# Norms between the stages of a diffusion backbone: VectorE squares the last two tiles, the root's table and the second block's split go early, the spread uses two banks, and an FFN's first two blocks are taken tile by tile

## The chip, the cores and the metric

The kernel runs on one core of a Trainium2 chip. The metric is the device time of one execution in microseconds (us); the time of a kernel is the median of several executions.

## The reference

A backbone of two layers works on 256 context tokens and 256 latent tokens of width 1024. Each layer is: half-step SwiGLU FFN, token mixer, half-step SwiGLU FFN. The mixer is an S5 state-space layer in layer 0 and a gated DeltaNet (GDN) in layer 1. Before each sub-layer stands an RMSNorm with a modulation that depends on the condition, and the output is normed once more:

```python
def rms_norm(x, g):
    xf = x.astype(jnp.float32)
    return xf * lax.rsqrt(jnp.mean(xf * xf, axis=-1, keepdims=True) + EPS) * g.astype(jnp.float32)

def ada_norm(x, g, shift, scale):
    return rms_norm(x, g) * (1.0 + scale) + shift

def swiglu(h, w13, w2):
    a, b = jnp.split(h @ w13, 2, axis=-1)
    return (jax.nn.silu(a) * b) @ w2
...
        x = x + 0.5 * mx[:, 2] * swiglu(ada_norm(x, norm_g[i, 0], mx[:, 0], mx[:, 1]), ffn_w13[i, 0], ffn_w2[i, 0])
```

In the last layer the context tokens stop after the mixer's input, so norms 5 and 6 and the last FFN work on the 256 latent tokens alone. Everything is float32.

## The kernel before

x lies in SBUF turned, as 8 tiles (KT) of 128 features x 512 tokens. Columns 0 to 255 are context, 256 to 511 latent. There are seven norms: m = 0 before FFN 0, 1 before S5, 2 before FFN 1 (behind the GLU that ends S5), 3 before FFN 2, 4 before GDN, 5 before FFN 3 (behind GDN's output projection "wo"), and 6 is the final one. Norms 5 and 6 have 256 columns.

**Products in three parts.** A float32 matrix product is made of three fast ones. Each operand is split in a high part (rounded) and a low part (the rest): whi and wlo for weights, hh and hl for activations, hidh and hidl for the FFN's hidden tiles. The products are hh x whi, hl x whi and hh x wlo. `mm3_pair` (L226 to L231) does them for one tile k of the input and two output tiles (the a and b columns of SwiGLU): six matmuls of 512 columns. A weight block has 2048 columns, in two halves of 1024, and a block of the first FFN product (`up`) is 8 tiles k, 48 matmuls. Blocks alternate between two slots, s = 0 and 1, of raw, whi and wlo. SyncE's queue loads raw once wlo's half of the slot's earlier block has been made (`load_halves`). ScalarE copies raw to whi (`split_hi`, L260), after TensorE has finished with the slot (blk_done), and VectorE subtracts to make wlo (`split_lo`, L266), which TensorE waits for. The function `blocks` sets the order on ScalarE and VectorE in each phase: split slot 1, work of slot 0, split slot 0 of the next pair, work of slot 1. So the first block of a phase is split at the end of the phase before, and its second block only after the norm that lies between.

**An FFN** has three parts p of 8, 8 and 6 hidden tiles, each with an up phase ("f1p0a": FFN 1, part 0) and a down phase ("f1p0b"). In the up phase ScalarE applies Silu (L568), VectorE multiplies by the gate (L597), GpSimd splits the hidden tile (L649, L651). In the down phase VectorE adds the products to x (`add_to_x`, L634), tile 4i + 2s from bank 4 and tile 4i + 2s + 1 from bank 5. In FFNs 1 and 2 VectorE also makes the modulation vectors of later norms by reductions, four to each block (L713), before the gate.

**A norm** m > 0 takes all engines in turn:
- GpSimd (`squares_pool`) squares tiles 0 to 6 as they are updated (L412) and adds them up in std (L421). ScalarE squares tile 7 (`root_act`, L323).
- TensorE (`norm_pe`, L376) sums both over partitions with the constant 1/1024, four quarters of the columns side by side, into bank 6.
- ScalarE takes the root (L330), with a table load ahead of it.
- VectorE takes the reciprocal (L428); TensorE spreads it over the partitions, again in four quarters, into bank 6 (`spread_pe`, L397).
- VectorE scales tile k into tmp (`scale`, L439), reading that bank for the first two tiles; ScalarE keeps a copy of it in SBUF (`keep_rstd`, L336) for the rest. ScalarE adds the shift and rounds to hh (L360); VectorE makes the low part hl (`low_part`, L451). TensorE's first block waits for the low part of tile k before its products of tile k.

Each engine works through its own instructions strictly in this written order, and semaphores tie the engines together. Norm 0 stands behind the loads and the preparation; there VectorE splits the first block's weights before the norm, and FFN 0 carries the S5 preparation (complex powers and tables) on all engines beside its matmuls. FFN 0 is written out instruction by instruction; most other phases are loops.

## Time and profile before

| | us |
|---|---|
| median of 3 runs | 2092.8 (2092.4 to 2093.47) |
| the profiled execution | 2093.45 |
| its span in the profile | 2091.6 |

| engine | busy us | share of the span |
|---|---|---|
| TensorE (PE) | 1968.2 | 94% |
| VectorE (DVE) | 1458.7 | 70% |
| ScalarE (ACT) | 710.6 | 34% |
| GpSimd (POOL) | 421.9 | 20% |

TensorE's granted clock was 0.978 of full speed over the span. In the profile's rows "idle before <-releaser" is how long the engine stood still before the group, and who ended that; "xN" is a count of instructions drawn as one row, and the time beside it is that of all N. The matmuls' ends are modelled and overlap the next one's start, so the pace of a stream is read from starts.

### The profile page before, as it was taken

Reading aid. Unit: us, or ns where it says so; the run is one execution under the profiler, and the core shown is the slowest. Engines: PE = TensorE matmul, PEld = TensorE weight load, DVE = VectorE, ACT = ScalarE, POOL = GpSimd, SP = SyncE. Lnnn points to the kernel's source line nnn. Section 1 sums busy time; section 2 is a strip of 40 time slices with the busy share of each in tenths; the row PEclk is TensorE's granted clock in tenths of the full one; section 3 lists DMA queues with packets and bytes.
Section 4 is the critical chain, followed back from the end, with each engine's and each line's share of the span. In section 5 each row is a group of like instructions: output and inputs, shape, how many; then the busy total and the mean of one; then the engine's idle time right before and its main releaser. Section 6 shows DMA issues by size and latency. Waiting matters only on the chain.

```text
span 2091.6 us, 37808 instructions
## 1 busy us (share of the span) xinstructions
PE 1968.2 (94%) x15026; PEld 1673.9 (80%) x15026; DVE 1458.7 (70%) x2353; ACT 710.6 (34%) x1138; POOL 421.9 (20%) x356
## 2 busy tenths in 40 slices
PE   5999999998998999999899999998999999879997
PEld 2778778777976788888678888886888988779997
DVE  7968778767645976858898586357677777655555
ACT  4222222223344322222242222225555555426332
POOL 0220110134722220202512021150000000022113
PEclk9999999998999999999999999998999999999999
DMA  8465665557633454544535453222011111015553
GB/s 330 161 243 200 207 222 203 199 167 290 236 121 121 160 176 146 186 136 156 185 121 181 141 188 113 96 86 85 29 45 52 42 43 62 23 61 169 180 177 97
DMA packets 85634, 305.06 MB, mean 146 GB/s; under 512 B 9856, under 2 KB 21632, under 8 KB 76032
## 3 DMA queue, kind: packets, MB, share of 16 engines
q1 hardware_dynamic: 80896, 285.41, 39.7%
q0 software_dynamic: 2304, 9.44, 1.1%
q10 hardware_dynamic: 2304, 8.39, 1.0%
q8 instruction: 93, 1.52, 0.3%
q14 instruction: 37, 0.30, 0.0%
HBM read 275.94 MB, written 27.26 MB: 145 GB/s over the span
## 4 chain that ended last, share of the span: by engine, by line
PE 82%; DVE 8%; ACT 3%; issue 2%; POOL 2%; DMA 2%; DVEq 1%; SPq 0%; ACTq 0%; POOLq 0%
PE PS L230 40%; PE PS L221 6%; PE PS L223 6%; PE PS L222 6%; PE PS L1722 6%; PE PS L1709 6%; DVE wlo L266 2%; PE PS L1306 1%; PE PS L684 1%; DMA et<-in_mod_w 1%; PE PS L1138 1%; DMA raw<-in_w_f0p0a 1%; POOL hidl L651 1%; PE PS L1112 1%; PE PS L1920 1%
## 5 line engine op out<-in xcount | busy, mean ns | idle before, releaser
L266 DVE TENSOR_TENSOR wlo<-raw,whi 128x1024 fp32r<-128x1024 f32 x314 | 451.2, 1477 | 83.7 <-ACT whi L260 81.9
L230 PE MATMUL PS<-hh,whi 128*128 128x512 f32 (+1 forms) x1536 | 443.3, 370 | 19.8 <-DVE hl L451 12.5
L230 PE MATMUL PS<-hl,whi 128*128 128x512 f32 (+1 forms) x1536 | 439.1, 367 | 0.0
L230 PE MATMUL PS<-hh,wlo 128*128 128x512 f32 (+1 forms) x1536 | 438.7, 367 | 0.0
L260 ACT ACTIVATE whi<-raw 128x1024 fp32r<-128x1024 f32 x300 | 301.2, 1052 | 276.9 <-PE PS L223 246.0
L230 PEld LDWEIGHTS PS<-hh,whi 128*128 128x128 f32 x1536 | 277.6, 191 | 73.5 <-issue 16.8
L230 PEld LDWEIGHTS PS<-hl,whi 128*128 128x128 f32 x1536 | 280.0, 191 | 47.1
L230 PEld LDWEIGHTS PS<-hh,wlo 128*128 128x128 f32 x1536 | 279.7, 191 | 47.1
L221 PE MATMUL PS<-hidh,whi 128*128 128x512 f32 (+1 forms) x704 | 257.9, 366 | 11.0 <-POOL hidl L651 8.3
L649 POOL CAST hidh<-gt 128x512 f32 (+2 forms) x88 | 63.0, 716 | 974.0 <-DVE gt L597 974.0
L222 PE MATMUL PS<-hidl,whi 128*128 128x512 f32 (+1 forms) x704 | 255.4, 363 | 0.0
L223 PE MATMUL PS<-hidh,wlo 128*128 128x512 f32 (+1 forms) x704 | 255.4, 363 | 0.0
L568 ACT ACTIVATE gt<-PS 128x512 f32<-128x512 f32 (+1 forms) x88 | 47.9, 545 | 568.2 <-PE PS L230 568.1
L713 DVE CUSTOM_DVE_ANT_0 junk<-modw,cb,modb 128x1024 f32<-128x1024 f32 x160 | 216.9, 1356 | 4.3
L634 DVE SCALAR_TENSOR_TENSOR x<-PS,hg,x 128x256 f32<-128x256 f32 (+1 forms) x176 | 77.9, 479 | 151.0 <-PE PS L223 148.6
L221 PEld LDWEIGHTS PS<-hidh,whi 128*128 128x128 f32 x704 | 132.9, 189 | 36.1 <-POOL hidl L651 11.0
L651 POOL TENSOR_TENSOR hidl<-gt,hidh 128x512 f32 (+2 forms) x88 | 157.0, 1785 | 13.2 <-POOL hidh L649 11.4
L223 PEld LDWEIGHTS PS<-hidh,wlo 128*128 128x128 f32 x704 | 132.9, 189 | 20.9
L222 PEld LDWEIGHTS PS<-hidl,whi 128*128 128x128 f32 x704 | 132.9, 189 | 19.7
L597 DVE TENSOR_TENSOR gt<-gt,PS 128x512 f32<-128x512 f32 (+1 forms) x88 | 54.6, 621 | 129.8 <-ACT gt L568 126.5
L2349 POOL TENSOR_TENSOR X<-BT,consts 128x256 f32<-128x256 f32 x16 | 13.6, 848 | 342.9 <-DVE BT L2192 342.9
L1722 PE MATMUL PS<-hh,whi 128*128 128x512 f32 (+1 forms) x256 | 72.2, 364 | 3.5 <-DVE hl L451 3.4
(344 smaller groups left out, 2597.9 us busy)
## 6 DMA issues: line engine op xcount, KB each, us to landing
modw<-in_mod_w SPq DMA_DIRECT2D x66, 1024.0 KB, 5.0
raw<-in_w_gdn SPq DMA_DIRECT2D x32, 512.0 KB, 3.9
cxd<-cx POOLq DMA_DIRECT2D x16, 576.0 KB, 7.2
cxS<-cxd SPq DMA_DIRECT2D x8, 1152.0 KB, 6.0
raw<-in_w_f0p0a SPq DMA_DIRECT2D x16, 512.0 KB, 7.5
vwd<-vws ACTq DMA_DIRECT2D x16, 512.0 KB, 6.6
raw<-in_w_f0p1a SPq DMA_DIRECT2D x16, 512.0 KB, 5.6
raw<-in_w_glu SPq DMA_DIRECT2D x16, 512.0 KB, 4.4
```

The source lines that it names most:

```text
L221: pe.matmul(dst, w_h, xh, start=first, stop=False)
L222: pe.matmul(dst, w_h, xl, start=False, stop=False)
L223: return pe.matmul(dst, w_l, xh, start=False, stop=last)
L230: ended = pe.matmul(dst, of[:, slot, c:c + P], moving, start=first and part_ == 0, stop=last and part_ == 2)
L260: act.activation(whi[:, s, c], raw[:, s, c], ACT.Copy).then_inc(whi_ready[half][s], 1)
L266: dve.tensor_tensor(wlo[:, s, c], raw[:, s, c], whi[:, s, c].bitcast(F32), ALU.subtract)\
L634: last = dve.scalar_tensor_tensor(out=xv, in0=pv, scalar=hg[:, layer, n, bass.ds(dt, 1), w:w + 1].rearrange("p a b -> p (a b)"), in1=xv, o ...
L649: pool.tensor_copy(hidh[:, bass.ds(2 * i + s, 1), c0:T], gt[:, s:s + 1, c0:T]).then_inc(hidh_ready[s], 1)
L651: pool.tensor_tensor(hidl[:, bass.ds(2 * i + s, 1), c0:T], gt[:, s:s + 1, c0:T], hidh[:, bass.ds(2 * i + s, 1), c0:T].bitcast(F32), ALU.su ...
L713: dve.tensor_tensor_reduce(out=junk[:, :], in0=modw[:, k % MS, D * j:D * j + D], in1=cb[:, w, :], scale=1.0, scalar=modb[:, layer, a:a + 1 ...
L1709: return pe.matmul(dst, lhsT, rhs, start=True, stop=True, tile_position=(SUB * at_row, SUB * at_col))
L1722: last = pe.matmul(PS[:, 2 * s + i, 0:T - c0], (whi, whi, wlo)[part_][:, s, (2 * k + i) * P:(2 * k + i + 1) * P], (hh, hl, hh)[part_][:, k ...
```

## The change

- The sum of squares: GpSimd now sums tiles 0 to 5 (one step fewer), and VectorE squares tiles 6 and 7 right behind their updates (`square_last`), with TensorE adding both in. ScalarE's square goes; instead it takes the root of one unused element first, which brings in the table.
- For norms 2, 3 and 5 (`FFN_AHEAD`) ScalarE splits the second block of the coming FFN before it waits for the sums; VectorE makes that block's low half 0 before the reciprocal and half 1 behind it.
- The reciprocal's spread goes to bank 7 for the context columns and bank 6 for the latent ones, with a signal after each half; the first scaling waits for its own half.
- In FFNs 1 to 3 the first two blocks are taken together: tiles 0 to 3 alternate between the blocks of slot 0 and slot 1, then tiles 4 to 7 of slot 0, then tiles 4 to 7 of slot 1. Where a product meets the norm, its order is hh x whi, hh x wlo, hl x whi, and only the last waits for the low part. FFN 0 gets that order for its first block, but not the pairing.
- Norm 0: GpSimd makes half 0 of the first block's low part, VectorE half 1 behind the first low part of the norm.
- VectorE's last down phase of each FFN and its GLU phase are written out, so that the squares can stand in them.

```diff
+NORM_BEHIND_FFN = [1, 3, 4, 6]
-SUM_STEPS = 1 + 2 * (KT - 2)
+SUM_STEPS = 1 + 2 * (KT - 3)
+FFN_AHEAD = {2: "f1p0a", 3: "f2p0a", 5: "f3p0a"}
...
+        def mm3_pair_low_last(pe, dsts, slot, cs, xh, xl, low, first, last):
+
+            for of, moving in ((whi, xh), (wlo, xh), (whi, xl)):
+                if moving is xl and low:
+                    pe.wait_ge(norm_done, low)
+                for dst, c in zip(dsts, cs):
+                    ended = pe.matmul(dst, of[:, slot, c:c + P], moving, start=first and of is whi and moving is xh, stop=last and moving is xl)
+            return ended
...
-            loop(eng, whole, written_out, one)
+            if ahead:
+                work(0, 0)
+                split(eng, 0, u0 + 1)
+                work(0, 1)
+            loop(eng, whole, written_out, one, int(ahead))
...
+        def spread_bank(m, w):
+            return sums_bank(m) if w else 7
...
-                for q in range(2):
-                    act.wait_ge(x_ready[q], 1 + X_BEFORE[m])
-                act.activation(tmp[:, KT - 1, c0:T], x[:, KT - 1, c0:T], ACT.Square).then_inc(sq_ready, 1)
+                act.activation(end[:, 0, 0:1], epst[:, 0:1], ACT.Sqrt)
+                if m in FFN_AHEAD:
+                    split_hi(act, 1, BASE[FFN_AHEAD[m]] // 2)
...
-            act.activation(rstd[:, c0:T], PS[:, sums_bank(m), c0:T], ACT.Copy).then_inc(rstd_kept, 1)
+            for w in halves(c0):
+                last = act.activation(rstd[:, cols(w)], PS[:, spread_bank(m, w), cols(w)], ACT.Copy)
+            last.then_inc(rstd_kept, 1)
...
-            pe.wait_ge(sq_ready, KT + m)
-            sums(tmp[:, KT - 1, :], False, True).then_inc(ss_ready, 1)
+            for q in range(2):
+                pe.wait_ge(sq_ready, KT + 2 * (m - 1) + q + 1)
+                last = sums(tmp[:, KT - 2 + q, :], False, q == 1)
+            last.then_inc(ss_ready, 1)
...
-            last.then_inc(rstd_spread, 1)
+                if q % 2:
+                    last.then_inc(rstd_spread, 1)
...
+        def square_last(dve, m, q):
+
+
+            c0 = NORMS[m][2] if m < len(NORMS) else CTX
+            dve.wait_ge(x_ready[q], 1 + X_BEFORE[m])
+            xv = x[:, KT - 2 + q, c0:T]
+            dve.tensor_tensor(tmp[:, KT - 2 + q, c0:T], xv, xv, ALU.mult).then_inc(sq_ready, 1)
...
+            if m in FFN_AHEAD:
+                split_lo(dve, 1, BASE[FFN_AHEAD[m]] // 2, (0,))
             dve.wait_ge(std_ready, m + 1)
             dve.reciprocal(rstd[:, 0:(T - c0) // 4], std[:, 0:(T - c0) // 4]).then_inc(rstd_ready, 1)
+            if m in FFN_AHEAD:
+                split_lo(dve, 1, BASE[FFN_AHEAD[m]] // 2, (1,))
             if m == 0:
...
-                split_lo(dve, 0, 0)
                 mods_take(dve, 0)
...
+                    if not kept and k == 0:
+                        dve.wait_ge(rstd_spread, 2 * m + w + 1)
...
             low_part(0)
+            if m == 0:
+                split_lo(dve, 0, 0, (1,))
...
+                def up_tile(i, s, k, meets_norm):
+                    if k == KT // 2:
+                        weights_in(pe, 1, s, BASE[a] // 2 + i)
+                    low = 0
+                    if meets_norm:
+                        pe.wait_ge(hh_ready, pieces_before(NORM_OF_FFN[f]) + len(halves(c0)) * (k + 1))
+                        low = made + len(halves(c0)) * (k + 1)
+                    return mm3_pair_low_last(pe, (PS[:, s, c0:T], PS[:, 2 + s, c0:T]), s, (2 * k * P, (2 * k + 1) * P),
+                                             hh[:, k, c0:T], hl[:, k, c0:T], low, k == 0, k == KT - 1)
...
+                def up_both():
+                    for s in range(2):
+                        up_begins(0, s)
+                    for k in range(KT // 2):
+                        for s in range(2):
+                            up_tile(0, s, k, s == 0)
+                    for s in range(2):
+                        for k in range(KT // 2, KT):
+                            last = up_tile(0, s, k, s == 0)
+                        up_ends(0, s, last)
...
-                loop(pe, n // 2, g, up)
+                ahead = p == 0 and f > 0
+                if ahead:
+                    up_both()
+                loop(pe, n // 2, g, up, int(ahead))
...
+                    last_slot = p == len(PARTS) - 1 and (i, s) == (1, 1)
+                    if last_slot:
+                        square_last(dve, NORM_BEHIND_FFN[f], 0)
...
         def _(pool):
             prime(pool, hid_ready)
+            split_lo(pool, 0, 0, (0,))
             ffn_pool(pool, 0)
```

## Rows read from the trace of the kernel before

**Rows 1.** The page: costliest lines of the chain that ended last.
```profile
PE PS L230 40%; PE PS L221 6%; PE PS L223 6%; PE PS L222 6%; PE PS L1722 6%; PE PS L1709 6%; DVE wlo L266 2%; PE PS L1306 1%; PE PS L684 1%; DMA et<-in_mod_w 1%; PE PS L1138 1%; DMA raw<-in_w_f0p0a 1%; POOL hidl L651 1%; PE PS L1112 1%; PE PS L1920 1%
```
**Rows 2.** Timeline of VectorE, norm 2: start us, us, engine line op, [idle before <-releaser].
```profile
662.66 1.27 DVE L1420 SCALAR_TENSOR_TENSOR x<-gt,hg,x 128x256 f32 x2 [0.25 <-DVE gt L1415]
666.36 0.95 DVE L428 RECIPROCAL rstd<-std 128x128 f32<-128x128 f32 x1 [2.44 <-ACT std L330]
669.56 1.65 DVE L439 SCALAR_TENSOR_TENSOR tmp<-x,gs,PS 128x256 f32<-128x256 f32 x4 [2.25 <-PE PS L397]
671.14 0.87 DVE L451 SCALAR_TENSOR_TENSOR hl<-tmp,mods,hh 128x256 fp32r<-128x256 f32 x2
...
686.15 2.36 DVE L266 TENSOR_TENSOR wlo<-raw,whi 128x1024 fp32r<-128x1024 f32 x2 [3.36 <-ACT whi L260]
```
**Rows 3.** Timeline of ScalarE, norm 2.
```profile
664.02 0.63 ACT L323 ACTIVATE tmp<-x 128x512 f32<-128x512 f32 x1 [2.51 <-DVE x L1420]
664.67 1.28 ACT L330 ACT_TABLE_LOAD   x1
...
685.08 1.98 ACT L260 ACTIVATE whi<-raw 128x1024 fp32r<-128x1024 f32 x2
```
**Rows 4.** Timeline of TensorE, norm 2 and the FFN's first three blocks.
```profile
667.37 2.08 PE L397 MATMUL PS<-rstd,consts 128*128 128x128 f32 x8 [2.24 <-DVE rstd L428]
672.15 1.19 PE L230 MATMUL PS<-hh,whi 128*128 128x512 f32 x2 [2.71 <-DVE hl L451]
...
687.42 0.73 PE L230 MATMUL PS<-hh,whi 128*128 128x512 f32 x2 [2.34 <-DVE wlo L266]
...
698.46 0.62 PE L230 MATMUL PS<-hh,whi 128*128 128x512 f32 x2
```
**Rows 5.** Windows: us, PE, PEld, DVE, ACT, POOL busy, PEclk, DMA share, GB/s.
```profile
672.15:687.42 15.27, 12.93 (x48) 10.15 (x48) 11.83 (x28) 11.39 (x19) 0.00 (x0) 0.88 0.00 1
```
**Rows 6.** Timeline of TensorE, norm 3: first, second and third block.
```profile
1049.35 1.19 PE L230 MATMUL PS<-hh,whi 128*128 128x512 f32 x2 [2.71 <-DVE hl L451]
...
1062.90 0.63 PE L230 MATMUL PS<-hh,whi 128*128 128x512 f32 x2
...
1073.81 0.62 PE L230 MATMUL PS<-hh,whi 128*128 128x512 f32 x2
```
**Rows 7.** Timelines of GpSimd and TensorE, norm 5.
```profile
1870.28 0.72 POOL L421 TENSOR_TENSOR std<-std,rstd 128x256 f32<-128x256 f32 x1
...
1876.55 0.77 PE L230 MATMUL PS<-hh,whi 128*128 128x256 f32 x2 [1.85 <-DVE hl L451]
...
1894.00 0.40 PE L230 MATMUL PS<-hh,whi 128*128 128x256 f32 x2
```
**Rows 8.** SyncE's issue of FFN 2's second block, and landing times around it.
```profile
1026.49 0.33 SPq L239 DMA_DIRECT2D raw<-in_w_f2p0a  x1
...
DMA to landing us min/median/max: 4.8/5.1/5.4
```
**Rows 9.** Timelines of VectorE and GpSimd before norm 4.
```profile
1399.02 3.21 DVE L266 TENSOR_TENSOR wlo<-raw,whi 128x1024 fp32r<-128x1024 f32 x2
...
1399.15 2.00 POOL L412 TENSOR_TENSOR rstd<-x 128x512 f32 x1 [1.25 <-DVE x L634]
...
1403.65 1.04 POOL L412 TENSOR_TENSOR rstd<-x 128x512 f32 x1 [0.27 <-POOL std L421]
```
**Rows 10.** Norm 0: VectorE's timeline, GpSimd's L651 (min/median/max ns), the chain.
```profile
35.92 2.36 DVE L266 TENSOR_TENSOR wlo<-raw,whi 128x1024 fp32r<-128x1024 f32 x2 [7.10 <-ACT whi L260]
...
38.42 0.18 DVE L737 SCALAR_TENSOR_TENSOR gs<-mods,ng 128x16 f32<-128x16 f32 x1
...
L651 POOL TENSOR_TENSOR hidl<-gt,hidh x22: 1296/2062/2067, 1071.7 to 1382.5; 128x512 f32 x22
...
66.23 1.15 DVE wlo L266
67.42 11.18 PE PS L230 x48
```

79 lines of the change are left out of this document (43 added, 36 removed).

## The prediction

> **What bounds the kernel.** I read the busy shares and the chain of waits first [rows 1]: TensorE is busy 94% of the span and the split matmuls of the up and gate projections alone are 40% of the chain that ended last. What can be won is where TensorE stands still or runs slowly. The timeline shows six such places, the norms between the stages; a seventh norm stands at the start. I read norm 2 (GLU to FFN 1) engine by engine as the pattern [rows 2 to 4], and norms 3 and 5 where they differ [rows 6, 7].
>
> In norm 2 the order is: last update of x (VectorE, to 663.93), ScalarE's square of tile 7, its table load of 1.28 us, the root at the end of that load, 665.96, the reciprocal at 666.36, TensorE's spread of 2.08 us, the scaling from 669.56, the first low part at 671.14, the first matmul of the FFN at 672.15, 9.5 us after VectorE began its last update [rows 2 to 4]. Then come two more losses. The granted clock over the first block is 0.88 [rows 5]: after the idle stretch its first four microseconds ran at the lower level, 1.2 GHz. And TensorE waits 2.34 us before the second block, whose table VectorE splits at 686.15, behind the whole norm [rows 2, 4]. A block at full clock takes 1073.81 - 1062.90 = 10.91 us; the first block of norm 3 took 13.55 with no wait in it, so the slow clock costs 2.64 us [rows 6].
>
> **Part 1: the sum of squares and the root.** VectorE squares tiles 6 and 7 itself. Tile 6 falls into its idle time before the last update, except in norm 3, where it pushes that update by about 0.35 us. Tile 7 is one TENSOR_TENSOR of 128x512. I price it at half of the 1.2 us of a 128x1024 split (2.36 for two), 0.6 to 0.7, plus about 0.25 for waiting on its own result (the idle before the last update of norm 2 shows that much): 0.93 against ScalarE's 0.09 + 0.63 = 0.72 [rows 2, 3]. So the sums come 0.2 later. The table load goes ahead of the wait, beside the last matmuls. The root began at 665.96; without the load it could begin after square (664.86), sums (0.43 on TensorE) and a hop: 665.4. That wins 0.6. Bounds: 0 (the load was hidden) and 1.28.
>
> **Part 2: the early split of the second block.** ScalarE's two copies (2.0 us, the last of [rows 3]) go before the wait on the sums. They need the slot free (TensorE's end, the same event that releases the last update) and the weights: the second half of norm 3's was issued at 1026.49 and such loads landed within 5.4 us, 8 us before they are needed [rows 8]. They end about 2 us after TensorE's end (later in norm 2, behind the table load: 664.8), when the sums are ready, so the root pays nothing. On VectorE the first half (1.2 us) stands before the reciprocal. With the square ending at 664.86 the reciprocal begins at 666.1 instead of 666.36: of the 0.6 only 0.3 is left in norm 2, 0.15 in norm 3. The second half (1.2) lies beside the first half of the spread and then delays the scaling by 0.1 to 0.2. Queued behind these VectorE instructions are only the reciprocal and the scaling; whoever waits for them is on the path, and that is counted.
>
> **Part 3: spread in two banks.** The context half can be scaled when half of the 2.08 us is done, and the keep on ScalarE becomes two copies, 0.1 us more, off the path. Scaling of the first tile: second half begins at 669.3 instead of 669.97. Full gain where nothing stands before it (norms 1 and 4): about 0.8. In norms 5 and 6 only one half exists, so nothing.
>
> **Part 4: first matmuls on the high part.** hh x whi and hh x wlo come before hl x whi, so TensorE starts when ScalarE's high part is there and no longer waits for VectorE's low part (1.0 us later). Four matmuls at the lower clock (about 0.43 each, twice the 0.227 of a fast one) cover it. Norm 2: reciprocal 666.1, second spread half 669.2, scaled 669.75, high part 670.3, TensorE at 670.4 instead of 672.15. Norm 3: 1047.65 instead of 1049.35.
>
> **Part 5: two blocks tile by tile.** 96 matmuls follow without a wait: 2 x 10.91 = 21.82 us plus 2.6 for the slow clock. VectorE makes a tile in 1.6 to 1.7 us (half of the four scalings' 1.65, and 0.87 for the low part, [rows 2]) and TensorE takes 2.73 over one now, so it is never starved. Norm 2: 670.4 + 21.8 + 2.6 = 694.8 against 698.46, **3.6 us**. Norm 3: 1047.65 + 24.4 = 1072.05 against 1073.81, **1.8** (no stall goes, only the late start). The clock's 2.64 stays and may be 1.6 or 3.2 each time, since I can't say when it rises.
>
> What is late next is the third block. Slot 0 is released after 12 of 16 tile-steps, 5.46 us before TensorE wants it again; formerly a whole block lay between. Chain: table load 1.28, Silu 0.6, first copy 1.05, split 1.2, together 4.3 with hops: it fits by 1.1 us in FFNs 1 and 2. VectorE's four reductions (5.4 us) stand before the gate, but begin when the norm ends and are over about when slot 0 is released.
>
> **Norm 5** has 256 columns: a block takes about 5.75 at full clock, a little over half. Before, GpSimd's sum ended at 1871.0, and all that follows hangs on it [rows 7]. Without tile 6 its sum ends one pair (1.75 us) earlier, at 1869.25; VectorE's squares, the second held up by GpSimd's last add, and the first split end at 1870.9, so the reciprocal begins then instead of 1.1 us after GpSimd's end, 1.15 earlier; the start on the high part 0.5 more: TensorE at 1874.9 instead of 1876.55. Slot 0 is free at 1874.9 + 2.2 (the slow clock, a little under norm 3's) + 8.6 = 1885.7; the third block needs 1.28 + 0.38 + 1.05 + 1.2 + hops after that, 1889.85, which is 1.2 after the pair is done: a new small wait. Before it started at 1894.00: **4.15**.
>
> **Norms 1, 4 and 6** have the root's 0.6 each; norm 1 adds the half spread at the quicker clock, **1.4**; norm 4 **1.1** (its first tiles are then paced by VectorE and ScalarE as now, so only the shift counts); the final norm has no split before the reciprocal, a square of half the width and no GpSimd sum at the end: **0.8**.
>
> **Norm 0.** VectorE's two splits (2.36 us from 35.92) go: the first half to GpSimd, the second behind the first low part. By VectorE's queue alone the scaling could start at 36.5 instead of 38.6. But [rows 9] show what happens when both engines read two SBUF operands: VectorE's two splits, 2.36 us alone (686.15, [rows 2]), took 3.21 beside GpSimd's square, and that took 2.00 instead of the 1.04 of another. The one waits while the other runs. GpSimd subtracts 128x512 in 1.30 us at best [rows 10], so 128x1024 in about 2.6: it holds from 35.85 to 38.4. The small instruction at 38.42 that makes gs has two SBUF operands and waits for that. So the scaling starts at 38.6 as before, and the second half of the split, 1.2 us, is now inside the norm. VectorE's queue runs 1.2 us later to the split at 66.23, for which TensorE waits until 67.42 [rows 10]. TensorE starts about 1 us earlier on the high part, which that wait takes back. I take **-1.0**; bounds -1.3 and +1.0 (no blocking: 2.1 won, 1.2 lost).
>
> The Trainium skill, SBUF — State Buffer ("Within the engine side, only the shared port pair causes contention"), says the pair is an exclusive lock which a VectorE instruction with two SBUF inputs and a GpSimd one hold for their whole length, the other blocking fully. The trace agrees (2.36 to 3.21, 1.04 to 2.00). By the lock norm 0 costs about 1; if the two ran side by side it would give up to 1.
>
> The same blocking could touch the squares, but GpSimd is done 0.1 to 3 us before them in norms 1 to 4; in norm 5 its last add costs VectorE about 0.4, which is counted.
>
> **The sum:** -1.0 + 1.4 + 3.6 + 1.8 + 1.1 + 4.15 + 0.8 = 11.85 us. The profiled execution took 2093.45 (span 2091.6 and 1.85 around it): 2081.6. It lies 0.65 above the median of the three runs, 2092.8, so the median comes to about **2081.0**. After each norm TensorE runs without longer waits to the next one, so nothing swallows the shift.
>
> **Rivals.** Faster or slower than what can be told from no change means by 0.2%, 4.2 us.
>
> A, the sum above: 0.66.
>
> B, the third block comes late everywhere. For: the margin of 1.1 us is that of one slow split (up to 3.2 for two beside GpSimd), and gate and reductions share VectorE. Against: in norm 2 the Silu table is already loaded, and GpSimd is idle then. If VectorE is in its reductions when slot 0 is released, TensorE waits up to 5 us in FFN 1 and FFN 2 and their 5.4 us are gone, with 1 more in FFN 3: about 2087.5. 0.14.
>
> C, the clock. It is low when the first matmuls of norm 2's block run, after the idle stretch. If the shorter gap keeps it up, or it rises at once, the three first pairs of blocks gain 2.6, 2.6 and 2.2: 2073.5. Against: 9 us without a stream remain. 0.07.
>
> D, slower: the straight code. 96 matmuls for each of three FFNs, GLU on VectorE and four last down phases are written out where loops were. If fetching it stopped an engine at each of some ten new stretches, it would decide from 1.2 us each for no gain and 1.7 for a loss of over 4 us: 2098. Against: FFN 0 is written out now, and there a block of 48 passes in 11.18 us, 0.27 above one in a loop [rows 6, 10]. 0.04.
>
> E, the norms don't shorten since the splits ahead of root and reciprocal eat all that the table and the square gave (ScalarE's copies last beyond the sums): only parts 4 and 5 stay, some 8 us less 1 at the start: 2085.5. 0.09.
>
> Below 2088.6 lie A, C, E and most of B: faster 0.93, within 0.2% 0.04, slower 0.03. The range of 8 in 10: from 2076 (clock 1.6 instead of 2.6 three times, norm 0 at +1.0) to 2087 (into B).
>
> **What would show it.** In the changed kernel's timeline: the table load before the root gone from between sums and root; reciprocal 0.2 to 0.3 us earlier against the last update in norms 2 and 3, over 1 in norm 5; first FFN matmul 7.7 us after the last update begins in norm 2 (now 9.5); 24.4 us for the first 96 pairs of FFN 1 and 2 without a wait; a wait of about 1 us before the third block in FFN 3 only; GpSimd's split ending near 38.4 and gs behind it. It would be wrong if TensorE waits before the third block in FFN 1 or 2, if the root starts later after the last update than now, or if block 2 of FFN 0 starts before 67.4.

## The result and the profile after

The changed kernel takes **2074.72 us** (median of 4 runs, 2070.94 to 2077.8) against 2092.81 for the kernel before beside it (4 runs, 2092.4 to 2093.47): ratio 0.9913, 95% interval 0.9898 to 0.9928. That is faster, as forecast (2081.0), but the time lies below the range of 2076 to 2087. The profiled execution took 2075.02 us with a span of 2073.2.

The page of the changed kernel, the span, its engines, and the costliest lines of the chain that ended last (answers to [rows 1]; line 242 is the former 230):

```profile
span 2073.2 us, 37686 instructions
PE 1971.4 (95%) x15074; PEld 1677.4 (81%) x15074; DVE 1473.1 (71%) x2364; ACT 690.8 (33%) x1128; POOL 412.7 (20%) x345
PE PS L242 38%; PE PS L223 6%; PE PS L224 6%; PE PS L225 6%; PE PS L1797 6%; PE PS L1784 6%; PE PS L232 4%; PE PS L1379 1%; DVE wlo L278 1%; PE PS L757 1%; DMA et<-in_mod_w 1%; PE PS L1211 1%; PE PS L1185 1%; POOL hidl L724 1%; PE PS L1995 1%
```

TensorE is what bounds it, as before. Norm 2, VectorE's timeline (columns: start us, us, engine, line, operation, out<-in, count, [idle before <-releaser]; answers to [rows 2]):

```profile
659.05 1.27 DVE L1493 SCALAR_TENSOR_TENSOR x<-gt,hg,x 128x256 f32<-128x256 f32 x2
660.36 0.69 DVE L459 TENSOR_TENSOR tmp<-x 128x512 f32<-128x512 f32 x1
660.97 1.22 DVE L278 TENSOR_TENSOR wlo<-raw,whi 128x1024 fp32r<-128x1024 f32 x1
662.10 0.94 DVE L467 RECIPROCAL rstd<-std 128x128 f32<-128x128 f32 x1
662.96 1.16 DVE L278 TENSOR_TENSOR wlo<-raw,whi 128x1024 fp32r<-128x1024 f32 x1
664.43 0.48 DVE L481 SCALAR_TENSOR_TENSOR tmp<-x,gs,PS 128x256 f32<-128x256 f32 x1 [0.31 <-PE PS L420]
```

Update, square, first half split, reciprocal, second half split follow each other with no idle time printed between them. The same stretch on ScalarE, whose table load now lies ahead of the update and beside nothing that waits for it (answers to [rows 3]):

```profile
658.25 1.28 ACT L340 ACT_TABLE_LOAD   x1
659.54 0.20 ACT L340 ACTIVATE consts_end<-epst 128x1 f32<-128x1 f32 x1
659.65 1.99 ACT L272 ACTIVATE whi<-raw 128x1024 fp32r<-128x1024 f32 x2
661.59 0.37 ACT L349 ACTIVATE std<-PS,epst 128x128 f32<-128x128 f32 x1
```

And TensorE, from the spread to the third block of FFN 1 (answers to [rows 4]); the 2.34 us of waiting before the second block is gone:

```profile
663.10 2.08 PE L420 MATMUL PS<-rstd,consts 128*128 128x128 f32 x8 [1.57 <-DVE rstd L467]
666.38 1.19 PE L242 MATMUL PS<-hh,whi 128*128 128x512 f32 x2 [1.21 <-ACT hh L381]
...
689.56 0.62 PE L242 MATMUL PS<-hh,whi 128*128 128x512 f32 x2
```

Norm 3 on TensorE (answers to [rows 6]). Its spread took 1.16 us, where norm 2's took 2.08:

```profile
1036.31 1.16 PE L420 MATMUL PS<-rstd,consts 128*128 128x128 f32 x8 [1.57 <-DVE rstd L467]
1038.86 1.19 PE L242 MATMUL PS<-hh,whi 128*128 128x512 f32 x2 [1.40 <-ACT hh L381]
...
1063.44 0.62 PE L242 MATMUL PS<-hh,whi 128*128 128x512 f32 x2
```

Norm 5, GpSimd, VectorE and TensorE (answers to [rows 7]):

```profile
1856.40 0.79 POOL L445 TENSOR_TENSOR std<-std,rstd 128x256 f32<-128x256 f32 x1
...
1858.53 0.54 DVE L467 RECIPROCAL rstd<-std 128x64 f32<-128x64 f32 x1
...
1861.57 0.77 PE L242 MATMUL PS<-hh,whi 128*128 128x256 f32 x2 [1.33 <-ACT hh L381]
...
1875.71 0.50 PE L242 MATMUL PS<-hh,whi 128*128 128x256 f32 x2
```

Norm 0 on GpSimd and VectorE (answers to [rows 10]): the tiny instruction that makes gs takes 1.96 us instead of 0.18 and ends at 38.3 with GpSimd's split.

```profile
35.93 2.35 POOL L278 TENSOR_TENSOR wlo<-raw,whi 128x1024 fp32r<-128x1024 f32 x1 [35.48 <-ACT whi L272]
...
36.35 1.96 DVE L810 SCALAR_TENSOR_TENSOR gs<-mods,ng 128x16 f32<-128x16 f32 x1
38.34 1.66 DVE L481 SCALAR_TENSOR_TENSOR tmp<-x,gs,PS 128x256 f32<-128x256 f32 x4
```

The milestones side by side, each from the timelines (before, after; us from the span's start), and what each norm gained by its own steps, counted from its own last update of x, beside the term of the prediction's sum:

| step | shift at its start | shift at its end | gained in it | predicted |
|---|---|---|---|---|
| norm 0 and FFN 0 | 0 | 469.80 to 470.23, +0.43 | -0.43 | -1.0 |
| norm 1, to the next stage's first operand | +0.43 | 476.57 to 475.20, -1.37 | 1.80 | 1.4 |
| stage between | -1.37 | 662.66 to 659.05, -3.61 | 2.24 | 0 |
| norm 2 and two blocks | -3.61 | 698.46 to 689.56, -8.90 | 5.29 | 3.6 |
| FFN 1's rest | -8.90 | 1039.94 to 1032.65, -7.29 | -1.61 | 0 |
| norm 3 and two blocks | -7.29 | 1073.81 to 1063.44, -10.37 | 3.08 | 1.8 |
| FFN 2's rest | -10.37 | 1414.39 to 1402.26, -12.13 | 1.76 | 0 |
| norm 4 | -12.13 | 1423.71 to 1409.79, -13.92 | 1.79 | 1.1 |
| stage between | -13.92 | 1866.79 to 1855.61, -11.18 | -2.74 | 0 |
| norm 5 and two blocks | -11.18 | 1894.00 to 1875.71, -18.29 | 7.11 | 4.15 |
| FFN 3's rest | -18.29 | 2077.55 to 2059.32, -18.23 | -0.06 | 0 |
| final norm | -18.23 | span 2091.6 to 2073.2, -18.4 | 0.17 | 0.8 |

The changed steps gave 18.81 us where 11.85 were predicted. The stages between lose and gain up to 2.7 us each and come to -0.41 together.

### The profile page after: what moved, and what is told of

It reads as the page before. It is cut to its first block, busy times and chain, and to the rows that moved or that the text cites. A ratio compares the mean times of both kernels' runs of the same rounds, so it can differ in the third digit from the quotient of the medians.

```text
span 2073.2 us, 37686 instructions
## 1 busy us (share of the span) xinstructions
PE 1971.4 (95%) x15074; PEld 1677.4 (81%) x15074; DVE 1473.1 (71%) x2364; ACT 690.8 (33%) x1128; POOL 412.7 (20%) x345
## 4 chain that ended last, share of the span: by engine, by line
PE 85%; DVE 8%; ACT 2%; issue 2%; DMA 1%; POOL 1%; SPq 1%; DVEq 0%; ACTq 0%; POOLq 0%
PE PS L242 38%; PE PS L223 6%; PE PS L224 6%; PE PS L225 6%; PE PS L1797 6%; PE PS L1784 6%; PE PS L232 4%; PE PS L1379 1%; DVE wlo L278 1%; PE PS L757 1%; DMA et<-in_mod_w 1%; PE PS L1211 1%; PE PS L1185 1%; POOL hidl L724 1%; PE PS L1995 1%
## 5 line engine op out<-in xcount | busy, mean ns | idle before, releaser
L242 PE MATMUL PS<-hh,whi 128*128 128x512 f32 (+1 forms) x1408 | 402.7, 368 | 9.1 <-ACT hh L381 7.9
L242 PE MATMUL PS<-hh,wlo 128*128 128x512 f32 (+1 forms) x1408 | 399.5, 365 | 0.0
L242 PE MATMUL PS<-hl,whi 128*128 128x512 f32 (+1 forms) x1408 | 399.1, 365 | 0.0
L242 PEld LDWEIGHTS PS<-hh,whi 128*128 128x128 f32 x1408 | 254.1, 191 | 56.6 <-issue 12.0
L242 PEld LDWEIGHTS PS<-hh,wlo 128*128 128x128 f32 x1408 | 255.6, 191 | 42.2
L242 PEld LDWEIGHTS PS<-hl,whi 128*128 128x128 f32 x1408 | 255.3, 191 | 42.4 <-DVE hl L493 0.6
L724 POOL TENSOR_TENSOR hidl<-gt,hidh 128x512 f32 (+2 forms) x88 | 161.3, 1832 | 12.6 <-POOL hidh L722 10.8
L224 PEld LDWEIGHTS PS<-hidl,whi 128*128 128x128 f32 x704 | 133.2, 189 | 19.9
L1797 PE MATMUL PS<-hh,whi 128*128 128x512 f32 (+1 forms) x256 | 72.7, 366 | 2.6 <-DVE hl L493 2.5
```

The source lines that it names most:

```text
L224: pe.matmul(dst, w_h, xl, start=False, stop=False)
L242: ended = pe.matmul(dst, of[:, slot, c:c + P], moving, start=first and of is whi and moving is xh, stop=last and moving is xl)
L724: pool.tensor_tensor(hidl[:, bass.ds(2 * i + s, 1), c0:T], gt[:, s:s + 1, c0:T], hidh[:, bass.ds(2 * i + s, 1), c0:T].bitcast(F32), ALU.su ...
L1797: last = pe.matmul(PS[:, 2 * s + i, 0:T - c0], (whi, whi, wlo)[part_][:, s, (2 * k + i) * P:(2 * k + i + 1) * P], (hh, hl, hh)[part_][:, k ...
```

## The experiments

Every kernel ran in 5 rounds beside the kernel before, whose medians were 2093.41, 2092.99 and 2092.29 us in the three groups. Median, range and ratio are of this kernel against that one. "First to third" is the time from the first matmul of an FFN to that of its third block, in the order FFN 1, 2, 3; before 26.31, 24.46, 17.45, after 23.18, 24.58, 14.14.

**The same kernel again (e1_same).**

> The changed kernel again, for its spread. Clock theory (what the prediction missed is mostly where TensorE's lower clock level happens to fall): its own times spread over several us (the four so far 2070.9 to 2077.8), the low stretches of this profile lie elsewhere than in the first one, and the steps of norms that hold no slow stretch repeat within 0.1 us. Rival (the missed 6.3 us are all the norms' own shorter steps): the times lie close to 2074.7 and the distances between the norms are those of the first profile within 0.5 us.

2073.5 (2072.29 to 2076.44), ratio 0.991 [0.9896, 0.9923]. The result stands. First to third was 24.60, 24.39, 12.88: FFN 1 and FFN 3 differ by more than a microsecond from the other execution of the same code. The way from the last update to the reciprocal (2.55, 3.05, 2.64, 2.55, 2.00 and 1.73 in norms 1 to 6, for norm 5 from the update's second instruction) and from there to the first operand or matmul of FFNs 1 to 3 repeats within 0.02 us. So the norms' own steps are firm and what follows them is not: both theories hold in part.

**Without the pairing (e2_no_pairing).** Blocks 1 and 2 one after the other, the rest as changed.

```diff
-                            last = up_tile(i, s, k, p == 0 and s == 0 and f == 0)
+                            last = up_tile(i, s, k, p == 0 and s == 0)
...
-                if ahead:
-                    up_both()
-                loop(pe, n // 2, g, up, int(ahead))
+                loop(pe, n // 2, g, up)
```

> The changed kernel with the first two blocks of FFNs 1 to 3 one after the other again (the low part still last for the first block; early split kept). If the pairing itself is worth little, because at the lower clock level TensorE takes 2.6 us over a tile and VectorE makes one in 1.6, so that the first block is hardly starved: the first 96 matmuls take 23 to 25 us in norms 2 and 3, and the time rises by 0 to 2 us. Rival, pairing is what wins: TensorE waits for the norm in the first block, 1.6 - 1.36 = 0.25 us a tile once the clock is up, and where the clock rises early it loses 2 us in each of the three FFNs: 4 to 6 us slower than the changed kernel.

2072.85 (2072.17 to 2075.97), ratio 0.9901 [0.9886, 0.9916], the same as with it. First to third 23.84, 24.36, 14.11. By itself, in this kernel, the pairing gives nothing measurable. FFN 2's first block took 13.48 us at a granted clock of 0.80 here.

**And the split behind the norm (e3_late_split).** As e2, and the second block is split where it was before.

```diff
+                split(eng, 1, u0)
...
-                if m in FFN_AHEAD:
-                    split_hi(act, 1, BASE[FFN_AHEAD[m]] // 2)
...
-            if m in FFN_AHEAD:
-                split_lo(dve, 1, BASE[FFN_AHEAD[m]] // 2, (0,))
...
-            if m in FFN_AHEAD:
-                split_lo(dve, 1, BASE[FFN_AHEAD[m]] // 2, (1,))
```

> As the one without pairing, and the second block's split behind the norm again, as before the change. TensorE should wait before the second block for VectorE's split: 2.3 us in norm 2 (ScalarE has another table and cb to do first), up to 1 in norm 3, 2 in norm 5, so 4 to 6 us over the kernel without pairing. In return the reciprocal should come up to 0.6 us earlier in norms 2, 3 and 5, for no split stands before it. Rival, the early split wins nothing of its own: within 1.5 us of it.

2080.11 (2077.96 to 2080.84), ratio 0.9934 [0.992, 0.9947]: 7.3 us slower than e2. First to third 28.99, 24.41, 15.05. TensorE's waits in this kernel between 666 and 698 us (columns: engine, what waited <- what released it: us in total, times, longest):

```profile
PE PS L242 <- DVE wlo L278: 3.3, 1, 3.3
```

The stall of [rows 4] is back, and longer. It also lowers the clock behind it: the second block ran at 0.86 and took 12.60 us, where the kernel before had it at 1.00 in 11.04 (687.42 to 698.46). The window of this second block:

```profile
684.36:696.96 12.60, 12.60 (x48) 10.24 (x49) 12.31 (x15) 2.01 (x3) 3.46 (x2) 0.86 0.39 134
```

Against e2 the early split is worth 5.2 us in FFN 1 (3.3 of waiting, the rest mostly this slower block) and 0.9 in FFN 3; in FFN 2 nothing.

**The old way to the root (e6_root_old).** The table load behind the square, tile 7 squared on ScalarE; tile 6 still on VectorE.

```diff
-                act.activation(end[:, 0, 0:1], epst[:, 0:1], ACT.Sqrt)
...
+                act.activation(tmp[:, KT - 1, c0:T], x[:, KT - 1, c0:T], ACT.Square).then_inc(sq_ready, 1)
...
+            if q:
+                return
```

> The changed kernel with ScalarE's square of tile 7 and its table load behind it again (GpSimd still sums only tiles 0 to 5, VectorE squares tile 6). By the prediction's price the root comes 0.6 us later, plus in norms 2, 3 and 5 up to 1.2, for the square now stands behind the two copies: 5 to 8 us slower than the changed kernel over six norms. Rival, most of the gain of the norms was GpSimd's shorter sum: within 2 us of it, except norm 3.

2080.92 (2076.84 to 2083.26), ratio 0.9938 [0.9924, 0.9951]: 7.4 us slower than e1. ScalarE's timeline of norm 2 in this kernel:

```profile
661.84 1.99 ACT L272 ACTIVATE whi<-raw 128x1024 fp32r<-128x1024 f32 x2
664.14 0.63 ACT L345 ACTIVATE tmp<-x 128x512 f32<-128x512 f32 x1 [0.32 <-DVE x L1498]
664.79 1.28 ACT L352 ACT_TABLE_LOAD   x1
666.09 0.37 ACT L352 ACTIVATE std<-PS,epst 128x128 f32<-128x128 f32 x1
```

From the last update to the reciprocal it takes 3.33, 3.73, 4.00 and 3.33 us in norms 1 to 4; after 2.55, 3.05, 2.66, 2.55. The table and the square are worth 0.68 to 1.34 us a norm on the path, 3.6 over four norms, with 0.94 in the last and 0.22 in norm 5. The rest of the 7.4 isn't seen in these steps; the spreads of norms 3 and 4 at the low clock (2.07 here, 1.16 and 1.52 after) hold 1.5 of it.

**The wait for the low part first (e10_low_first).**

```diff
-                        pe.wait_ge(hh_ready, pieces_before(NORM_OF_FFN[f]) + len(halves(c0)) * (k + 1))
-                        low = made + len(halves(c0)) * (k + 1)
+                        pe.wait_ge(norm_done, made + len(halves(c0)) * (k + 1))
...
-                    return mm3_pair_low_last(pe, (PS[:, s, c0:T], PS[:, 2 + s, c0:T]), s, (2 * k * P, (2 * k + 1) * P),
+                    return mm3_pair(pe, (PS[:, s, c0:T], PS[:, 2 + s, c0:T]), s, (2 * k * P, (2 * k + 1) * P),
-                                             hh[:, k, c0:T], hl[:, k, c0:T], low, k == 0, k == KT - 1)
+                                             hh[:, k, c0:T], hl[:, k, c0:T], k == 0, k == KT - 1)
```

> The changed kernel with TensorE waiting for the low part of each tile before it begins on it, hl x whi in second place, pairing kept. The prediction had 1.0 us for each of norms 2 and 3 and 0.5 for 5, 2.5 us in all; the first FFN matmul should come 1.0, 1.0 and 0.5 us later after the reciprocal. Rival, the clock gives it back or takes more: 0 or 5 us.

2076.56 (2071.58 to 2077.93), ratio 0.9919 [0.9905, 0.9932]. From reciprocal to first matmul 5.32, 4.64, 3.56 us (after 4.28, 3.55, 3.04): 1.04, 1.09 and 0.52, together 2.65 of the 3.1 by which its median is above e1's. The ranges overlap, so the mechanism rests on the rows, not on the medians.

**The spread in one bank (e9_one_bank).**

```diff
-            return sums_bank(m) if w else 7
+            return sums_bank(m)
...
-                        dve.wait_ge(rstd_spread, 2 * m + w + 1)
+                        dve.wait_ge(rstd_spread, 2 * m + 2)
```

> The changed kernel with the spread in one bank again, so that the first scaling waits for all of it. By the prediction it costs 0.8 us in norms 1 and 4 and 0.7 in 2 (at the lower clock), less in norm 3, nothing in 5 and 6: 2 us slower. If the clock is up during a spread (1.16 us in all), half of it is 0.6 and VectorE's second half split covers it: 0 to 1 us. Rival: nothing at all within 1 us, since the context half's scaling is followed by the latent half's wait anyway.

2073.18 (2069.74 to 2076.61), ratio 0.9908 [0.9893, 0.9923], no difference. Reciprocal to scaling grew as it should, 2.27, 3.18, 2.45, 3.20 in norms 1 to 4 (after 1.83, 2.33, 1.94, 1.83), some 3.2 us in all. Where they were given back I can't name; first to third was 24.38, 24.03, 12.93. The split in two banks is right in the trace and not resolved in the time.

**The kernel before with its loops written out (e7_written_out).** VectorE's last down phases and the GLU phase, nothing else.

```diff
-                blocks(dve, b, split_lo, update, g)
+                blocks(dve, b, split_lo, update, g or p == len(PARTS) - 1)
...
-            blocks(dve, "glu", split_lo, glu)
+            blocks(dve, "glu", split_lo, glu, True)
```

> The kernel before with one thing alone: VectorE's last down phase of each FFN and its GLU phase written out. The stage from norm 1 to norm 2 was 2.24 us shorter in the changed kernel's first profile, though nothing of the norm lies in it. Theory: 0.25 us of it is VectorE's wait for its own result in the loop, the rest is where the clock's low stretches fell in the S5 stage; so 0 to 1.5 us faster than before, and the 0.25 us wait before the last update of norm 2 is gone. Rival, the loops cost 0.5 us or more a turn: 3 us or more faster.

2092.07 (2090.55 to 2097.79, 12 runs), ratio 1.0001 [0.9991, 1.0011]. Nothing, either way: neither the cost of rival D nor a gain. Update to reciprocal is that of before in norms 1 to 4 (3.31, 3.70, 3.61, 3.31), so the shorter way comes from the moved instructions.

**Idle matmuls in the norms (e4_warm).** The clock was priced as given. Here TensorE gets matmuls that nobody reads, into the bank of the first block, which that block overwrites: after the sums, after the spread, and between the sums of tiles 6 and 7.

```diff
+        def warm(pe, n):
+            for _ in range(n):
+                pe.matmul(PS[:, 0, :], const("eye"), consts[:, 0:4, :].rearrange("p a b -> p (a b)"), start=True, stop=True)
...
+                if q == 0:
+                    warm(pe, {1: 1, 2: 3, 3: 1, 4: 1, 6: 1}.get(m, 0))
...
+            warm(pe, {1: 1, 2: 1, 3: 1, 4: 1, 5: 1, 6: 1}.get(m, 0))
...
+            if m:
+                warm(pe, {2: 1, 3: 1, 4: 1, 5: 1}.get(m, 0))
```

> The changed kernel with 15 further matmuls of 128x512 float32 on TensorE into a free bank, whose output nothing reads: one after the sums and one after the spread of each norm, and one (three in norm 2) between the sums of tiles 6 and 7; each 0.85 us at full clock, into gaps of 1.1 to 3.1 us. Clock theory: the gaps shrink to under 1 us each, the granted clock falls later or not at all in the norms, a spread takes 1.1 instead of 2.1 us and the first 96 matmuls of FFNs 1 and 2 take nearer 21.8 than 24.4: 3 to 10 us faster than the changed kernel. Rival, the level falls whatever short work stands in the gaps: the low stretches stay where they are and each norm is 0 to 0.5 us longer, 0 to 3 us slower.

2067.29 (2063.01 to 2068.89), ratio 0.9872 [0.9856, 0.9888]: 6.2 us under e1, with no overlap of ranges: the clock theory, within its 3 to 10. The edit issues 17 of them, each recorded as a pair that takes about 1.1 us; these numbers hold where an expectation has others. TensorE in norm 2 of this kernel:

```profile
664.02 1.13 PE L391 MATMUL PS<-consts 128*128 128x512 f32 x2
665.67 1.16 PE L427 MATMUL PS<-rstd,consts 128*128 128x128 f32 x8 [0.52 <-DVE rstd L476]
666.66 1.02 PE L391 MATMUL PS<-consts 128*128 128x512 f32 x2
668.22 0.70 PE L242 MATMUL PS<-hh,whi 128*128 128x512 f32 x2 [0.54 <-ACT hh L381]
```

The spread takes 1.16 us instead of 2.08, and the first pair 0.70 instead of 1.19. The windows of norm 2 (columns: us, then busy time and count of PE, PEld, DVE, ACT and POOL, the granted clock, DMA share, GB/s), first after, then e4_warm, where the second row holds exactly the first 96 matmuls:

```profile
656.80:667.00 10.20, 4.29 (x37) 3.04 (x36) 8.05 (x13) 5.89 (x10) 0.00 (x0) 0.77 0.53 183
666.38:689.56 23.18, 23.18 (x96) 19.07 (x97) 20.22 (x41) 12.60 (x21) 2.52 (x2) 0.94 0.16 58
```

```profile
659.00:669.00 10.00, 8.58 (x51) 4.21 (x49) 8.11 (x13) 6.03 (x11) 0.00 (x0) 1.00 0.46 159
668.22:690.07 21.85, 21.85 (x96) 18.04 (x97) 18.90 (x40) 12.60 (x21) 1.42 (x1) 1.00 0.16 47
```

First to third 21.85, 21.86, 11.95: what the prediction gave for two blocks at full clock is 21.82.

**The same without the pairing (e5_warm_no_pairing)**, the edit of e2 on e4.

> The kernel with the 15 idle matmuls (2067.3), its pairing undone. Theory: pairing was worth nothing only because the slow clock hid VectorE's pace. With the clock up, TensorE takes 1.36 us over a tile of the first block and VectorE 1.6, so the first block of FFNs 1 and 2 is starved by about 0.25 us a tile and that of FFN 3 (0.72 against 1.05) by 0.3: the first 96 matmuls take 24 instead of 22.3 in norms 2 and 3, and the time rises by 4 to 6 us. Rival, pairing is worthless at either clock: no difference beyond 1.5 us.

2069.57 (2067.66 to 2071.07), ratio 0.989 [0.9875, 0.9904], 2.3 above e4. First to third 23.79, 23.69, 13.60: 1.94, 1.83 and 1.65 more than with the pairing, 5.4 together in the profile, of which only 2.3 arrives in the median, under the 4 to 6 expected; the two ranges overlap, so this too rests on the rows. FFN 2's first block took 12.81 us at a granted clock of 1.00, that is VectorE's pace of 1.6 us a tile. With the clock up the pairing does what it could not do at the low one. The idle matmuls give 3.3 us without the pairing (2072.85 in e2 to 2069.57) and 6.2 with it.

**More of them (e8_warm2).**

```diff
-                    warm(pe, {1: 1, 2: 3, 3: 1, 4: 1, 6: 1}.get(m, 0))
+                    warm(pe, {1: 1, 2: 4, 3: 1, 4: 1, 6: 1}.get(m, 0))
...
-            warm(pe, {1: 1, 2: 1, 3: 1, 4: 1, 5: 1, 6: 1}.get(m, 0))
+            warm(pe, {1: 2, 2: 2, 3: 2, 4: 2, 5: 2, 6: 1}.get(m, 0))
...
-                warm(pe, {2: 1, 3: 1, 4: 1, 5: 1}.get(m, 0))
+                warm(pe, {1: 3, 2: 1, 3: 1, 4: 2, 5: 2}.get(m, 0))
...
+            warm(pe, 5)
```

> More idle matmuls than in the first kernel of this kind (34 instead of 15, 0.56 us each by its trace): 5 before FFN 0, two after the sums, 1 to 3 after the spread, so that norm 5, norm 1 and the start are covered too. Theory: norm 5's low stretch, still there at 1852.7 to 1856.1 with the spread at 1.79 us, goes; the start's second low stretch shrinks; 1 to 4 us faster than 2067.3. Rival: they now delay the spread (two of them last 1.1 us, the reciprocal comes 1.6 after the sums) or the first block, and it is 0 to 3 us slower.

2068.15 (2065.45 to 2068.65), ratio 0.9878 [0.9864, 0.9892], not told apart from e4; the gain of 1 to 4 didn't come. The edit issues 33. Those after the sums now hold up the spread as the rival has it: it begins 1.28 to 1.29 us after the reciprocal in norms 1, 2 and 4, where e4 has 1.01.

**The kernel before with idle matmuls (e12_before_warm).**

```diff
+            warm(pe, {2: 4}.get(m, 0))
             sums(tmp[:, KT - 1, :], False, True).then_inc(ss_ready, 1)
+            warm(pe, 3 if m < 5 else 1)
...
+            warm(pe, {1: 3, 2: 3, 3: 3, 4: 3, 5: 2}.get(m, 0))
```

> The kernel before the change with idle matmuls alone (three after the sums of each norm, three after the spread, four between GpSimd's sum and tile 7 in norm 2). Clock theory: its spreads take 1.1 to 1.3 instead of 2.08 us and its first blocks come near 12.9 us, VectorE's pace, instead of 13.5 to 15.3; 4 to 9 us faster than before. Rival, the clock's cost in the norms is an effect of the changed kernel only, or the gaps of 9.5 us are too long to be filled: within 2 us of before.

2091.85 (2088.53 to 2095.81, 12 runs), ratio 0.9998 [0.9988, 1.0008]: no gain in the time. First to third 26.33, 24.45, 15.28: in FFNs 1 and 2 those of before to 0.02 us, though the clock is full (in FFN 3, where the first pair of matmuls still took 1.42 us, it is 2.2 less, which the medians don't show). The window of FFN 2's first block in this kernel, then TensorE's rows in it:

```profile
1048.38:1061.81 13.43, 12.69 (x49) 8.44 (x49) 11.80 (x28) 9.60 (x18) 0.00 (x0) 1.00 0.00 1
```

```profile
1050.18 0.73 PE L230 MATMUL PS<-hh,whi 128*128 128x512 f32 x2 [0.17 <-DVE hl L458]
...
1051.81 0.74 PE L230 MATMUL PS<-hh,whi 128*128 128x512 f32 x2
...
1061.81 0.73 PE L230 MATMUL PS<-hh,whi 128*128 128x512 f32 x2 [0.54 <-DVE wlo L266]
```

The tiles begin 1.63 us apart (and 1.61 to the next, at 1053.42), the 1.6 to 1.7 in which VectorE makes one, not the 1.36 that TensorE needs for its six matmuls of 0.227. From the first block's first matmul to the second's it takes 13.43 us at clock 1.00; in the kernel before it took 13.55 at 0.80 [rows 6]. Of the 13.43, 12.89 go at the pace of the tiles, and the last 0.54 are a wait for VectorE's split of the second block, which stands behind the whole norm. So those 2.64 us over a fast block are VectorE's, by its pace and its late split, and the slow clock had only hidden them.

That is shown for FFNs 1 and 2 alone. The experiment isn't a clean one elsewhere: its own idle matmuls hold up the spread, above all in norm 3, where it begins 2.14 us after the reciprocal instead of 1.01:

```profile
1041.94 2.84 PE L370 MATMUL PS<-consts 128*128 128x512 f32 x6
1044.62 1.05 PE L403 MATMUL PS<-rstd,consts 128*128 128x128 f32 x8
```

In norm 5 the spread is still at the low clock (1.97). From the reciprocal to the first operand or matmul the profile gained 0.32, 0.65 and 0.66 us in norms 1, 2 and 4, and lost 0.10 and 0.68 in 3 and 5; with FFN 3's 2.2 that is some 3 us which the medians don't show. Fewer idle matmuls, placed so that they delay nothing, were not tried in this kernel.

**All but norm 0 (e11_warm_norm0).** e4 with norm 0 as before and 4 idle matmuls more behind the spreads.

```diff
-            split_lo(pool, 0, 0, (0,))
...
-            if m == 0:
-                split_lo(dve, 0, 0, (1,))
...
+                split_lo(dve, 0, 0)
                 mods_take(dve, 0)
...
-                warm(pe, {2: 1, 3: 1, 4: 1, 5: 1}.get(m, 0))
+                warm(pe, {1: 3, 2: 1, 3: 1, 4: 2, 5: 1}.get(m, 0))
```

> The changed kernel with 18 idle matmuls (those of the first such kernel, two more after norm 1's spread and one more after norm 4's) and norm 0 as it was before the change, VectorE splitting both halves first. Theory of the blocked port: norm 0's way over GpSimd costs 0.5 us, measured from ScalarE's rows at 34.3 to the split before FFN 0's third block, so this is 0.5 to 1 us faster than 2067.3, the fastest so far. Rival: GpSimd's half pays by TensorE's earlier start, 0 to 0.5 slower.

2065.38 (2063.12 to 2068.12), ratio 0.9873 [0.9857, 0.989]. It has the lowest median of all, but its range overlaps that of e4, so the 0.5 to 1 us expected isn't resolved in the time. The part undone is seen in the trace: from ScalarE's activation just ahead of its split copies (33.76 us here) to the low part that lets block 2 of FFN 0 begin it takes 31.95 us before and 31.99 here, 32.40 to 32.42 in after, e1 and e4. GpSimd's half costs 0.4 us. VectorE here, with gs short again:

```profile
35.40 2.36 DVE L278 TENSOR_TENSOR wlo<-raw,whi 128x1024 fp32r<-128x1024 f32 x2 [6.51 <-ACT whi L272]
37.68 0.18 DVE L807 TENSOR_TENSOR mods<-PS,modb 128x32 f32<-128x32 f32 x1
37.90 0.17 DVE L818 SCALAR_TENSOR_TENSOR gs<-mods,ng 128x16 f32<-128x16 f32 x1
38.10 1.66 DVE L491 SCALAR_TENSOR_TENSOR tmp<-x,gs,PS 128x256 f32<-128x256 f32 x4
```

## Why the direction was right and the number wrong

The changed steps gave 6.96 us more than predicted. They divide so, each from the timelines of before and after:

| from, to | norms | predicted | measured |
|---|---|---|---|
| last update, reciprocal | 1 to 6 | 0.6, 0.3, 0.15, 0.6, 1.15, 0.6 = 3.4 | 0.76, 0.65, 0.95, 0.76, 2.41, 0.92 = 6.45 |
| reciprocal, first matmul or operand | 1 to 5 | 0.8, 1.45, 1.55, 0.5, 0.5 = 4.8 | 1.04, 1.51, 2.25, 1.03, 1.39 = 7.22 |
| first matmul, third block | 2, 3, 5 | 1.85, 0.1, 2.5 = 4.45 | 3.13, -0.12, 3.31 = 6.32 |
| final norm's rest | 6 | 0.2 | -0.75 |
| norm 0 | 0 | -1.0 | -0.43 |

The first two rows hold 5.47 of the 6.96. On the side of the changed kernel e1 repeats them within 0.02 us, but for norm 4's second term (0.12) and what is said of norm 5 below, so they don't hang on one execution of it. The third row's terms do: in e1 they are 1.71, 0.07 and 4.57. The lower end of the forecast was made of the clock and norm 0 alone; the norms' own steps, where the miss lay, stood in it as fixed.

**The step that failed most is the norms' way to the reciprocal, parts 1 and 2 and norm 5's GpSimd term: 3.4 us forecast, 6.45 measured.** In its own words: "of the 0.6 only 0.3 is left in norm 2, 0.15 in norm 3". The mechanism held and the size was off. The square was given 0.25 us of waiting for its own input and the sums and hops were stacked behind it. In the trace VectorE's square begins 0.04 us after the updates end and the first half of the split begins before the square's row ends, so update, square and split take 3.05 us to the reciprocal instead of the 3.44 I had. Norm 3 gained 0.95 where 0.15 stood. e6 gives the price of table and square by undoing them: 0.78, 0.68, 1.34, 0.78 in norms 1 to 4. That the splits ahead of the reciprocal eat the gain (rival E) fell with that: ScalarE's root in norm 2 starts at 661.59, 0.07 after the sums end.

The Trainium skill, ScalarE: Activation LUTs ("What ACT_TABLE_LOAD costs"), puts a switch of tables at about 1283 ns of load and about 1380 ns of drain, 2.66 us in all. The load agrees (1.28). Of the drain this trace shows nothing: the next activation begins at 659.54, where the load of 658.25 ends, in the kernel before the load began 0.02 after the square's end [rows 3], and putting the load and the square back on the path (e6) cost 0.68 to 1.34.

**Norm 5's 1.15** came out as 2.4. GpSimd's sum ended 4.2 us after the first of VectorE's last updates began and now ends 1.6 after it, 2.6 earlier where I had one pair, 1.75. The other 0.9 is the pair of tile 5, which formerly began 1.04 us after that update (1867.83) and now 0.10 after it (1855.71). Part of this belongs to the one profile of before: there GpSimd was late from an earlier collision, an add of 1.67 us (1862.43) beside VectorE's split of 2.90 (1862.28). In e7, whose norms are those of before, the add takes 0.74 and the split 2.36, tile 5's pair begins 0.50 after the update, and the way from update to reciprocal is 4.57 us (4.58 in e12) where before has 5.33. Against e7 norm 5's step gained 1.65, not 2.41; the term was still too small, by 0.5 instead of 1.26. The reciprocal then waits for VectorE's own square and split, 1.34 us behind GpSimd's end, where I had 1.7. The 0.4 us that GpSimd's last add was to cost VectorE's second square isn't there: the square begins 0.03 after its update and takes 0.44 (0.42 in the final norm, where GpSimd is done). No run puts tile 6 back on GpSimd alone, so this share rests on the rows; e6, which keeps it, gives back only 0.22 of the 2.41.

**"The clock's 2.64 stays" is wrong in its reading**, and this is the instructive one. I read the 13.55 us of norm 3's first block as the lower clock's cost. e12 gives that block full clock and it still takes 13.43 to the second block, since VectorE feeds it and splits the next one behind it. Two limits lay on each other, and the trace of before could have told it: the pace of 1.6 to 1.7 us a tile times 8 tiles is 13.2, and it stood in my own text beside the 2.73. In the changed kernel the pairing and the early split lift VectorE's limit, and the clock alone is left, which is why the forecast of 24.4 came out all the same: 24.58 us in FFN 2 and 24.60 in FFN 1 of e1, 23.18 in FFN 1 of after, 21.85 with the clock held up (e4).

**The low clock is not a constant of the norm.** In the second row of the table, norm 3 gained 2.25 instead of 1.55, and norm 5 1.39 instead of 0.5, since the spread ran before the clock fell: 1.16 and 1.10 us instead of 2.08 and 1.97. Its price of 2.08 was taken from the norms as long as they were. For norm 3 that goes with the length of the norm: the spread takes 1.16 to 1.40 us in after, e1, e2, e3, e9 and e10, and 2.07 in e6, whose way to the reciprocal is 1.34 longer, and 1.90 in e7. In norms 1, 4 and 6 it changes from one execution to the next; the final norm's 1.85 instead of 1.10, which makes its -0.75, is 1.10 in e1. Rival C was right in kind: a shorter norm can give back clock, 0.9 in a spread. The 1.2 in FFN 1's pair of blocks came in one of two executions, and nothing like 2.6, 2.6 and 2.2. That its 2073.5 lies beside the measured 2074.72 is luck: the time came from the steps. I gave it 0.07 and kept it apart from A; it belonged into A's range.

**What the pairing is worth**: nothing at the low clock (e2), as the 1.8 forecast for norm 3 ("no stall goes, only the late start") implies. Norm 2's own 3.13 (1.71 in e1) is the removed stall (e3: 5.15 with the split put back, of which 3.3 waiting) and belongs to the early split. The pairing's 2.3 us show only with the full clock (e5).

**The third block in FFN 3 waited 0.05 us, not 1.2.** The chain I summed had the Silu table's 1.28 us behind slot 0's end. In the trace the load is issued when the norm's last activation ends and is done before TensorE is:

```profile
1867.99 0.51 ACT L381 ACTIVATE hh<-tmp,mods  x1 [0.49 <-DVE tmp L481]
1868.52 1.28 ACT L636 ACT_TABLE_LOAD   x1
1872.99 0.38 ACT L636 ACTIVATE gt<-PS 128x256 f32<-128x256 f32 x1 [3.19 <-PE PS L242]
```

Here the load did not wait for TensorE, as the activation behind it did (in FFN 2 the load is at 1049.65, the activation at 1058.20). Rival B fell: TensorE printed no wait at the third block in FFN 1 or 2. It was nearer in FFN 1 than I had it, since VectorE's reductions waited for ScalarE's cb until 680.56 and ended at 685.84, 1.5 us after ScalarE's Silu had begun. Whether the early root of an unused element is needed in norms 1, 4 and 6, where no copy stands behind it, was not tested.

**Norm 0**: the mechanism is as predicted. GpSimd's half ends at 38.28 (38.4 forecast) and gs, two SBUF operands, stretches from 0.18 to 1.96. The price is 0.43 in the profile and 0.4 in e11, not 1.0. The Trainium skill, SBUF — State Buffer ("SBUF: two separate sides"), calls the port pair that VectorE and GpSimd share an exclusive lock. The trace agrees here down to an instruction of 16 columns: it ends at 38.31, with GpSimd's.

**Rival D fell**: e7 wrote the loops out and measured 1.0001 [0.9991, 1.0011]. TensorE's written-out blocks have no run of their own, but in e4 the pairs take 21.85 and 21.86 us where two looped blocks would take 21.82, which leaves no room for a stop.

**The stages between** were taken as 0, and their sum is, -0.41; singly they are not. The granted clock over 478 to 600 us was 0.94 before and 0.96 after, and the stage that it lies in took 2.24 us less. Between two executions of the same kernel the first to third differs by up to 1.4 us, and its times by 6.9 (2070.94 to 2077.8). What sets where the clock falls in those stages is open; idle matmuls there were not tried. Open too is the rest of e6's 7.4 us (its rows give 4.7 to the reciprocals and 1.5 to spreads, and the runs of either kernel spread over 4 to 6 us) and where e9's 3.2 us went.

Put together from pairs of experiments, in medians: root and table 7.4 (e6), early split 7.3 (e3 against e2), low part last 3.1 (e10), two banks and pairing 0 (e9, e2), norm 0 -0.4 (e11's rows), 17.4 of the 18.1 to 19.9 measured. The sum is a loose one: GpSimd's shorter sum has no experiment, and e6's 7.4 is more than its rows show.

## What to carry to other kernels

When a stretch runs at a low clock, compare its length with the pace of whoever feeds it before blaming the clock: two limits can give the same duration, and then removing one gives little until the other is gone (idle matmuls: 0 in the kernel before, 3.3 us in the changed one without the pairing, 6.2 with it). A serial head such as a norm can pay twice when it is shortened, since after a shorter idle stretch of TensorE the last small matmuls may still run at full clock (norm 3's spread: 1.16 instead of 2.08), and a few matmuls that nobody reads take what is left, if they stand where they delay nothing. Prices of steps inside such a head, read at the low clock, are not constants.
